# Operand splits of the fourth to sixth weight slab moved between the x parts at the start of three layers

## The chip, the cores and the metric

The kernel runs on one core of one Trainium2 chip. The metric is device time in microseconds (us) of one execution. Engines: TensorE (PE; its weight loads are PEld), VectorE (DVE), ScalarE (ACT), GpSimd (POOL) and the queue of SyncE (SP), which issues the loads.

## The reference, cut to what matters

Three blocks of token mixing alternate with three PEER layers (expert retrieval), over 256 tokens of width 1024. Each PEER layer begins with a norm of its input and a query projection; from the queries come scores against keys, the best 16 of each half, and then the experts' products.

```python
h = layer_norm(DN_ALPHA * h + mix, ln_g[layer, 0], ln_b[layer, 0])     # layers 0 and 1
ffn = peer(h, peer_w_q[layer], peer_sub_keys[layer], peer_u[layer], peer_v[layer])
...
h = h + peer_ffn(rmsnorm(h, g_ffn[l]), w_q[l], sub_keys[l], expert_u[l], expert_v[l])   # the third

q = (xt @ w_q).reshape(T, PEER_HEADS, 2, PEER_HALF)                    # 1024 x 2048 weights
```

The change lies wholly in the seam between the norm and `xt @ w_q`, in each of the three layers.

## The kernel before, in words

**Products.** Every fp32 product is made of three: an operand is split into a part `hi` (rounded to the matmul's format) and a rest `lo`, and hi\*hi, hi\*lo and lo\*hi are summed (`split_matmuls`, lines 598 to 600).

**Slabs.** All weights stream through a ring of three slots as slabs of 128 x 1024 (512 KB). A slab n goes through this chain: SyncE loads it into `ring` once the slot's previous `w_lo` is made (`put`, line 393); ScalarE makes `w_hi` (`split_lead`, line 903), once it is loaded and once slab n-3 is used up by TensorE (semaphore `used`); GpSimd or VectorE makes `w_lo = ring - w_hi` (`split_rest`, line 549); TensorE waits for `w_lo` (`slab_ready`). Which engine makes `w_lo` is written out by hand for each stretch: in the query slabs it is GpSimd, in `gpsimd_program`'s `peer`.

**A PEER layer's start.** The first eight query slabs (here slabs 0 to 7 of the layer) go through `wide`: slab c holds 128 rows of `w_q`, and x feature chunk c is the stationary operand. There are two tiles of 128 tokens, each with two halves of 512 columns, so a slab takes 6 products of 512 columns for one tile and 12 for both. `used` is raised when tile 1's products of the slab are done. Slabs 0 to 3 need features 0 to 511 of x (half 0), slabs 4 to 7 need half 1. Queries 8 to 15 come after them, with products of 256 columns.

**x.** The normed activations lie by token. TensorE turns them (a transpose through the identity, line 701, four for one part into a bank `acc`), ScalarE copies the part out as `x_hi` (`lead_x`, line 939), and VectorE makes `x_lo` (`rest_part`, line 1287). The four parts (tile, half) come in the order of `SKEW`: part 0 is (0,0), part 1 (1,0), part 2 (0,1), part 3 (1,1).

**The order before.** On TensorE (`skewed_queries`): turn part 0; slabs 0, 1 for tile 0; turn part 1; slab 2 for tile 0; slabs 0, 1, 2 for tile 1; turn parts 2 and 3; slab 3 and then slabs 4 to 7 for both tiles. On ScalarE (`finish`): `w_hi` of slabs 0 to 2 and `x_hi` of part 0, squares and standard deviation of tile 1, `x_hi` of parts 1, 2, 3, and only then (`peer`, `leads(first, DC)`) `w_hi` of slabs 3 and on. On VectorE (`skewed_layer_norm` in the first two layers, `skewed_rms` in the third): the norm's steps with `x_lo` of parts 0 and 1 between them, then `x_lo` of parts 2 and 3. On GpSimd: `w_lo` of slabs 0 to 15 in order. On SyncE (`sync_program`'s `peer`): slabs 0 to 5; then, once the whole input is normed, four loads of keys with three slabs after each. Every engine runs its own instructions in order.

Of the kernel before, what the change touches and what calls it, by code (L numbers as in the profile page):

```python
# [29 lines left out]
DC = D // P  # L30
# [4 lines left out]
SLOTS = 3  # L35
# [4 lines left out]
HP = 2 * HEADS  # L40
# [6 lines left out]
SKEW = ((0, 0), (1, 0), (0, 1), (1, 1))  # L47
# [505 lines left out]
def gpsimd_program(k, pool):  # L553
    def run(name, at, rounds):

        with pool.Fori(0, rounds) as i:
            for p in range(SLOTS):
                split_rest(k, pool, Slab(k.first[name] + at + p, i))

    def some(name, at, to):  # L560
        for n in range(at, to):
            split_rest(k, pool, Slab(k.first[name] + n))

    def stage(name, count):
        run(name, 0, count // SLOTS)
        some(name, count - count % SLOTS, count)

    def peer(layer):
        stage(f"qw{layer}", HP)
        u = f"u{layer}"  # L570
        run(u, 0, (EARLY + SLOTS) // SLOTS)
        some(u, (EARLY + SLOTS) // SLOTS * SLOTS, EARLY + SLOTS)

    for name in k.stages:
        if name[:4] == "peer":
            peer(int(name[4]))
        else:
            for part in PARTS_OF[name]:
                part = f"{name}_{part}"
                if part in ("ab_wide", "c_wide"):  # L580
                    continue
                if k.first[part]:
                    stage(part, k.count[part])
                else:
                    some(part, 1, k.count[part])
# [5 lines left out]
class Tensor:  # L591
# [100 lines left out]
    def skewed_queries(self, layer, src):  # L692

        k, pe, w = self.k, self.pe, self.w
        first, parts, banks = k.first[f"qw{layer}"], k.parts_before(f"peer{layer}"), k.query_banks()

        def turn(n):
            t, half = SKEW[n]
            pe.wait_ge(k.h_part, parts - 4 + n + 1)
            for c in range(4):  # L700
                ins = pe.transpose(k.acc[t * 2 + half][:, c * P:(c + 1) * P],
                                   src[t][:, (4 * half + c) * P:(4 * half + c + 1) * P], k.ident[:, :])
            ins.then_inc(k.xt, 1)

        def slabs(*chunks, tiles=range(NT)):
            for c in chunks:
                self.wide(Slab(first + c), c, banks, tiles=tiles)

        self.keep_busy(20)
        turn(0)  # L710
        self.keep_busy(12)
        w.next(k.x_ready)
        slabs(0, 1, tiles=[0])
        turn(1)
        slabs(2, tiles=[0])
        w.next(k.x_ready)
        slabs(0, 1, 2, tiles=[1])
        turn(2)
        turn(3)
        slabs(3)  # L720
        w.next(k.x_ready, 2)
        slabs(4, 5, 6, 7)
# [165 lines left out]
class Scalar:  # L888
# [78 lines left out]
    def tile_squares(self, t):  # L967
# [4 lines left out]
            self.square(k.h[:, t, half * 512:(half + 1) * 512], 2 * t + half)  # L972
        self.tile_std(t)

    def finish(self, name, end):

        k, act = self.k, self.act
        after = k.stages[k.stages.index(name) + 1:][:1]
        act.activation(k.small[:, 46:47], k.small[:, 47:48], ACT.Sqrt)
        if after == ("s",):  # L980
            self.w.next(k.meta, 16)
            self.square(MixS(k).meta, 2 * NT)
            self.tile_std(NT)
        self.split_lead(Slab(end))
        if name in RMS_AFTER:
            self.tile_squares(0)
            if after:
                self.split_lead(Slab(end + 1))
                self.split_lead(Slab(end + 2))
                self.lead_x([0], halves=[0])  # L990
            self.tile_squares(1)
            if after:
                for t, half in SKEW[1:]:
                    self.lead_x([t], halves=[half])
            return
        eps = k.small[:, 49:50]
        if after in (("peer0",), ("peer1",)):
            self.centred_squares(0)
            self.tile_std(0, eps)
            self.split_lead(Slab(end + 1))  # L1000
            self.split_lead(Slab(end + 2))
            self.lead_x([0], halves=[0])
            self.centred_squares(1)
            self.tile_std(1, eps)
            for t, half in SKEW[1:]:
                self.lead_x([t], halves=[half])
        elif after != ("s",):
            for t in range(NT):
                self.centred_squares(t)
            for t in range(NT):  # L1010
                self.tile_std(t, eps)
            self.split_lead(Slab(end + 1))
            self.lead_x([0])
            self.lead_x([1])
            self.split_lead(Slab(end + 2))
        else:
            for t in range(NT):
                self.centred_squares(t)
                if t:
                    self.tile_std(0, eps)  # L1020
                self.split_lead(Slab(end + 1 + t))
            self.tile_std(1, eps)
            self.lead_meta()
            for t in range(NT):
                self.tile_squares(t)
            self.lead_x(range(NT), at=META)

    def peer(self, layer):
# [20 lines left out]
            bank = k.query_bank(n)  # L1049
            self.column(Slab(first + n), q[:, n, :], src=None if bank is None else lambda _: bank[:, 0:T])  # L1050

        self.leads(first, DC)
        self.wide(first + DC - 1, [(k.query_banks()[t * 2 + half], q_tok[:, t, half * 512:(half + 1) * 512], ACT.Copy)
                                   for t in range(NT) for half in range(2)], k.q_tok)
        for n in range(DC, HP):
# [115 lines left out]
class Vector:  # L1171
# [118 lines left out]
    def skewed_layer_norm(self, slot, last):  # L1290
        k, dve, own = self.k, self.dve, self.own
        gain, bias = view(k.big, G_AT[slot], D), view(k.big, G_AT[slot] + D, D)
        means, squares, before = self.w.count(k.mean), self.w.count(k.sq), self.w.count(k.xhi)

        def residual(t, half):
            self.add_residual(t, half, last, DN_ALPHA, sums=True)

        def minus_mean(t):
            own.join()
            dve.tensor_scalar(k.small[:, 20 + t:21 + t], k.small[:, 16 + 2 * t:17 + 2 * t],  # L1300
                              k.small[:, 17 + 2 * t:18 + 2 * t], -1.0 / D, ALU.add, ALU.mult).then_inc(k.mean, 1)

        def centre(t, half):
            dve.wait_ge(k.mean, means + t + 1)
            dve.wait_ge(k.sq, squares + 2 * t + half + 1)
            acc = k.acc[t * 2 + half][:, :]
            own.do(dve.scalar_tensor_tensor(acc, acc, k.small[:, 20 + t:21 + t], gain[:, half * 512:(half + 1) * 512],
                                            ALU.add, ALU.mult))

        def variance(t):  # L1310
            dve.wait_ge(k.sq, squares + 2 * t + 2)
            dve.tensor_scalar(k.small[:, 4 + t:5 + t], k.small[:, 40 + 2 * t:41 + 2 * t],
                              k.small[:, 41 + 2 * t:42 + 2 * t], 1.0 / D, ALU.add, ALU.mult).then_inc(k.var, 1)

        def scale(t, half):
            cut, acc = slice(half * 512, (half + 1) * 512), k.acc[t * 2 + half][:, :]
            own.join()
            dve.scalar_tensor_tensor(k.h[:, t, cut], acc, k.small[:, 12 + t:13 + t], bias[:, cut], ALU.mult, ALU.add)\
               .then_inc(k.h_part, 1)

        residual(0, 0)
        residual(0, 1)
        minus_mean(0)
        residual(1, 0)
        self.w.next(k.param[slot], 32)
        centre(0, 0)
        variance(0)
        self.inverse_std(0)
        scale(0, 0)
        residual(1, 1)  # L1330
        minus_mean(1)
        self.rest_part(0, before)
        centre(1, 0)
        variance(1)
        self.inverse_std(1)
        scale(1, 0)
        centre(0, 1)
        self.rest_part(1, before)
        scale(0, 1)
        centre(1, 1)  # L1340
        scale(1, 1)
        self.rest_part(2, before)
        self.rest_part(3, before)
        self.w.skip(k.mean, 2)
        self.w.skip(k.sq, 4)
        self.w.skip(k.xhi, 4)
        self.w.skip(k.h_part, 4)

    def skewed_rms(self, last):
# [7 lines left out]
        def normed(t, half):  # L1357
            cut = slice(half * 512, (half + 1) * 512)
            dve.wait_ge(k.rms_in, parts + 2 * t + half + 1)
            dve.scalar_tensor_tensor(view(k.big, NORMED + t * D + half * 512, 512), k.h[:, t, cut],  # L1360
                                     k.small[:, 12 + t:13 + t], view(k.big, G_AT[0], D)[:, cut],
                                     ALU.mult, ALU.mult).then_inc(k.h_part, 1)
# [13 lines left out]
        normed(0, 1)  # L1376
        self.rest_part(1, before)
        normed(1, 1)
        self.rest_part(2, before)
        self.rest_part(3, before)  # L1380
        self.w.skip(k.rms_in, 4)
# [1674 lines left out]
```

## Time and profile before

| | us |
|---|---|
| median of 3 runs | 2921.48 |
| range of the runs | 2921.19 to 2923.51 |
| profiled execution, its own device time | 2923.99 |
| its span in the trace | 2922.2 |
| TensorE busy (99% of the span) | 2879.9 |
| VectorE busy (66%) | 1937.0 |
| ScalarE busy (54%) | 1564.6 |
| GpSimd busy (31%) | 894.1 |

The mean granted clock of TensorE over the span is 0.996. Times in the trace are us from the span's start. A timeline row gives start, duration, engine, line, operation, what it writes and reads, how often, and in brackets how long the engine stood idle before it and what ended that. L598, L599 and L600 are the three products of `split_matmuls`. A matmul's duration is longer than the distance to the next, because they overlap: the pace is read from the starts.

### The profile page before, as it was taken

The numbers are of one execution on the slowest core, as the hardware profiler recorded it, in microseconds if no ns is written. First come the engines' busy times: TensorE is split into PE (matmuls) and PEld (weight loads), VectorE is DVE, ScalarE is ACT, GpSimd is POOL, SyncE is SP. The second block draws the span as 40 slices with busy tenths as digits, with TensorE's granted clock in tenths as the row PEclk, the third lists the DMA queues.
The fourth block names the chain that finished last, engine by engine and source line by source line (L and its number), as shares of the span: only waits on it lengthen the run. The fifth ranks groups of instructions, "written<-read, shape, count | busy, mean of one in ns | idle before, by whom it ended". The sixth has DMA issues, their size and how long they took to land.

```text
span 2922.2 us, 59257 instructions
## 1 busy us (share of the span) xinstructions
PE 2879.9 (99%) x21307; PEld 2618.0 (90%) x21307; DVE 1937.0 (66%) x3382; ACT 1564.6 (54%) x2548; POOL 894.1 (31%) x361
## 2 busy tenths in 40 slices
PE   8999999999999999999999999999999999999999
PEld 7799999888888879999998888889799999988887
DVE  4379477788556636947778855675529667788655
ACT  4444544677555544454467744654554544477554
POOL 3679600000004367970000000255779820000000
PEclk9999999999999999999999999999999999999999
DMA  6556555555765455565555576433466555555664
GB/s 214 160 174 182 186 168 172 173 173 179 238 191 163 145 158 174 186 185 169 171 172 174 178 234 196 144 130 123 162 182 181 181 181 168 170 175 177 203 195 162
DMA packets 146462, 515.17 MB, mean 176 GB/s; under 512 B 17552, under 2 KB 18576, under 8 KB 146336
## 3 DMA queue, kind: packets, MB, share of 16 engines
q1 hardware_dynamic: 146336, 513.46, 56.0%
q8 instruction: 83, 1.36, 0.2%
q14 instruction: 43, 0.35, 0.0%
HBM read 509.20 MB, written 4.19 MB: 176 GB/s over the span
## 4 chain that ended last, share of the span: by engine, by line
PE 91%; POOL 2%; DVE 2%; ACT 2%; issue 2%; DMA 0%; SPq 0%; DVEq 0%; ACTq 0%; POOLq 0%
PE col L598 15%; PE col L600 15%; PE col L599 15%; PE acc L598 13%; PE acc L600 13%; PE acc L599 13%; POOL w_lo L549 2%; PE col L796 2%; PE acc L796 2%; PE acc L754 1%; ACT w_hi L903 1%; ACT work L963 0%; PE acc L2511 0%; PE misc L2524 0%; DVE work L1840 0%
## 5 line engine op out<-in xcount | busy, mean ns | idle before, releaser
L549 POOL TENSOR_TENSOR w_lo<-ring,w_hi 128x1024 fp32r<-128x1024 f32 x357 | 893.9, 2515 | 1461.3 <-ACT w_hi L903 1460.2
L903 ACT ACTIVATE w_hi<-ring 128x1024 fp32r<-128x1024 f32 x941 | 992.8, 1056 | 571.9 <-PE acc L600 449.2
L598 PE MATMUL col<-x_hi,w_hi 128*128 128x256 f32 (+1 forms) x3712 | 1051.8, 283 | 2.9 <-DVE x_lo L1192 1.7
L599 PE MATMUL col<-x_lo,w_hi 128*128 128x256 f32 (+1 forms) x3712 | 1045.3, 282 | 0.0
L600 PE MATMUL col<-x_hi,w_lo 128*128 128x256 f32 (+1 forms) x3712 | 1044.9, 281 | 0.0
L549 DVE TENSOR_TENSOR w_lo<-ring,w_hi 128x1024 fp32r<-128x1024 f32 x584 | 714.0, 1223 | 375.1 <-ACT w_hi L903 371.7
L598 PEld LDWEIGHTS col<-x_hi,w_hi 128*128 128x128 f32 x3712 | 701.4, 189 | 6.2 <-issue 3.3
L600 PEld LDWEIGHTS col<-x_hi,w_lo 128*128 128x128 f32 x3712 | 702.4, 189 | 0.0
L599 PEld LDWEIGHTS col<-x_lo,w_hi 128*128 128x128 f32 x3712 | 698.7, 188 | 0.7
L598 PE MATMUL acc<-w_hi,c_hi 128*128 128x512 f32 x1664 | 653.5, 393 | 1.0 <-issue 1.0
L600 PE MATMUL acc<-w_hi,c_lo 128*128 128x512 f32 x1664 | 648.2, 390 | 0.0
L599 PE MATMUL acc<-w_lo,c_hi 128*128 128x512 f32 x1664 | 647.4, 389 | 0.0
L910 ACT ACTIVATE work<-col 128x256 f32 (+1 forms) x431 | 166.0, 385 | 663.6 <-PE col L600 663.5
L600 PEld LDWEIGHTS acc<-w_hi,c_lo 128*128 128x128 f32 x1664 | 312.3, 188 | 66.1
L598 PEld LDWEIGHTS acc<-w_hi,c_hi 128*128 128x128 f32 x1664 | 312.5, 188 | 64.4 <-issue 1.5
L599 PEld LDWEIGHTS acc<-w_lo,c_hi 128*128 128x128 f32 x1664 | 312.6, 188 | 63.3
L1450 DVE TENSOR_TENSOR c_lo<-work,c_hi 128x256 fp32r<-128x256 f32 x390 | 165.2, 424 | 14.4 <-ACT c_hi L1097 14.1
L1097 ACT ACTIVATE c_hi<-work 128x256 fp32r (+1 forms) x384 | 153.6, 401 | 0.0
L1457 DVE MAX8 work<-work 128x8 f32<-128x128 f32 (+1 forms) x144 | 35.4, 322 | 161.4 <-ACT work L1038 161.1
L1583 DVE SCALAR_TENSOR_TENSOR work<-acc,work 128x512 f32 (+1 forms) x96 | 61.8, 686 | 99.9 <-PE acc L796 99.9
L1572 DVE TENSOR_TENSOR h_tok<-mask_i,pairs_of_gate 128x2048 f16<-128x2048 f16 x96 | 123.6, 1287 | 0.0
L1102 ACT ACTIVATE h_tok<-iota_fp,neg_i 128x128 f16<-128x128 f16 x384 | 121.9, 388 | 0.2
(326 smaller groups left out, 2184.5 us busy)
## 6 DMA issues: line engine op xcount, KB each, us to landing
ring<-in_u SPq DMA_DIRECT2D x384, 512.0 KB, 3.5
ring<-in_v SPq DMA_DIRECT2D x384, 512.0 KB, 3.5
ring<-in_qw SPq DMA_DIRECT2D x24, 512.0 KB, 3.5
ring<-in_wq SPq DMA_DIRECT2D x24, 512.0 KB, 3.6
ring<-in_s_in SPq DMA_DIRECT2D x21, 512.0 KB, 3.3
ring<-in_c_in SPq DMA_DIRECT2D x16, 512.0 KB, 3.6
ring<-in_s_out SPq DMA_DIRECT2D x16, 512.0 KB, 3.3
ring<-in_s_gate SPq DMA_DIRECT2D x12, 512.0 KB, 3.3
```

The source lines that it names most:

```text
L549: eng.tensor_tensor(k.w_lo[s.slot][:, :], k.ring[s.slot][:, :], k.w_hi[s.slot][:, :].bitcast(F32), ALU.subtract).then_inc(k.lo[s.slot], 1)
L598: pe.matmul(out, a[0], b[0], start=start, stop=False, **kw)
L599: pe.matmul(out, a[0], b[1], start=False, stop=False, **kw)
L600: return pe.matmul(out, a[1], b[0], start=False, stop=stop, **kw)
L796: ins = pe.matmul(banks[t // HALF][:, t % HALF * EARLY:(t % HALF + 1) * EARLY], k.oh1[:, t, :], k.oh2[:, n, t, :], start=n == 0, stop=n == ...
L903: act.activation(k.w_hi[s.slot][:, :], k.ring[s.slot][:, :], ACT.Copy).then_inc(k.hi[s.slot], 1)
L910: act.activation(dst, src, func).then_inc(k.evac, 1)
L1097: act.activation(k.c_hi[s.slot][:, :], act_of[:, s.index(values), :], ACT.Copy).then_inc(k.coef_h, 1)
L1102: act.activation(k.oh1[:, t, :], k.iota_b[:, :], ACT.Abs, bias=k.neg_i1[:, at])\
L1450: dve.tensor_tensor(k.c_lo[s.slot][:, :], src, k.c_hi[s.slot][:, :].bitcast(F32), ALU.subtract).then_inc(k.coef[s.slot], 1)
L1572: dve.tensor_tensor(k.oh2.rearrange("p n t (i two) -> p n t i two", two=2), mask.unsqueeze(1).to_broadcast(shape), k.gate[:, bass.ds(b.ind ...
L1583: ins = dve.scalar_tensor_tensor(part, banks[half][:, :].rearrange("p (t i) -> p i t", t=HALF), 1.0 / GATE_UNIT, part, ALU.mult, ALU.mult)
```

## The change

Four edits, the same in all three PEER layers.

- TensorE turns part 2 after slab 0's products for tile 1 (then slab 1), and part 3 after slab 1's (then slab 2), not both after slab 2's.
- ScalarE makes `w_hi` of slab 3 after `x_hi` of part 1, of slab 4 after part 2's and of slab 5 after part 3's (`leads_among_x`); `leads` in `peer` begins with slab 6 accordingly.
- VectorE makes `w_lo` of slab 3, between the last step of the norm and `x_lo` of part 2.
- GpSimd leaves slab 3 out; it makes slabs 0 to 2 and 4 to 15, written out rather than in a loop.

```diff
     def peer(layer):                                   # gpsimd_program
-        stage(f"qw{layer}", HP)
+        some(f"qw{layer}", 0, SLOTS)
+        some(f"qw{layer}", SLOTS + 1, HP)
...
         w.next(k.x_ready)                              # skewed_queries
-        slabs(0, 1, 2, tiles=[1])
+        slabs(0, tiles=[1])
         turn(2)
+        slabs(1, tiles=[1])
         turn(3)
+        slabs(2, tiles=[1])
         slabs(3)
         w.next(k.x_ready, 2)
         slabs(4, 5, 6, 7)
...
+    def leads_among_x(self, end):                      # Scalar
+        for n, (t, half) in enumerate(SKEW[1:]):
+            self.lead_x([t], halves=[half])
+            self.split_lead(Slab(end + SLOTS + n))
...
-            for t, half in SKEW[1:]:                   # finish, at both places
-                self.lead_x([t], halves=[half])
+            self.leads_among_x(end)
...
-        self.leads(first, DC)                          # Scalar.peer
+        self.leads(first + SLOTS, DC - SLOTS)
...
         scale(1, 1)                                    # skewed_layer_norm
+        split_rest(k, dve, Slab(last + 1 + SLOTS))
         self.rest_part(2, before)
...
         normed(1, 1)                                   # skewed_rms
+        split_rest(k, dve, Slab(last + 1 + SLOTS))
         self.rest_part(2, before)
```

## Rows read from the trace of the kernel before

**Rows 1.** The page: busy us, share of the span and instructions of each engine
```profile
PE 2879.9 (99%) x21307; PEld 2618.0 (90%) x21307; DVE 1937.0 (66%) x3382; ACT 1564.6 (54%) x2548; POOL 894.1 (31%) x361
```
**Rows 2.** TensorE's waits over the span: us in total, times, longest
```profile
PE col L598 <- POOL w_lo L549: 13.2, 7, 4.1
```
**Rows 3.** Timeline of TensorE, first PEER layer
```profile
100.88 0.60 PE L701 MATMUL acc<-ident,h_tok 128*128 128x128 f32 x4
101.23 0.48 PE L598 MATMUL col<-w_hi,x_hi 128*128 128x512 f32 x1
101.55 0.39 PE L599 MATMUL col<-w_lo,x_hi 128*128 128x512 f32 x1
...
104.38 0.40 PE L598 MATMUL col<-w_hi,x_hi 128*128 128x512 f32 x1
...
107.18 1.03 PE L701 MATMUL acc<-ident,h_tok 128*128 128x128 f32 x8
...
112.33 0.79 PE L598 MATMUL col<-w_hi,x_hi 128*128 128x512 f32 x1 [4.11 <-POOL w_lo L549]
...
128.77 0.28 PE L598 MATMUL acc<-x_hi,w_hi 128*128 128x256 f32 x1
```
**Rows 4.** Timeline of ScalarE, same layer
```profile
107.82 1.08 ACT L939 ACTIVATE x_hi<-acc 128x512 fp32r<-128x512 f32 x2 [5.71 <-PE acc L701]
108.79 2.95 ACT L903 ACTIVATE w_hi<-ring 128x1024 fp32r<-128x1024 f32 x3
117.85 1.06 ACT L903 ACTIVATE w_hi<-ring 128x1024 fp32r<-128x1024 f32 x1 [6.11 <-PE misc L600]
```
**Rows 5.** Timeline of VectorE and GpSimd, same layer
```profile
104.19 0.75 DVE L1318 SCALAR_TENSOR_TENSOR h_tok<-acc,small,work 128x512 f32<-128x512 f32 x1
108.45 1.29 DVE L1287 TENSOR_TENSOR x_lo<-acc,x_hi 128x512 fp32r<-128x512 f32 x2 [3.50 <-ACT x_hi L939]
...
95.82 4.73 POOL L549 TENSOR_TENSOR w_lo<-ring,w_hi 128x1024 fp32r<-128x1024 f32 x2 [4.08 <-ACT w_hi L903]
109.92 7.00 POOL L549 TENSOR_TENSOR w_lo<-ring,w_hi 128x1024 fp32r<-128x1024 f32 x3 [9.37 <-ACT w_hi L903]
118.99 2.40 POOL L549 TENSOR_TENSOR w_lo<-ring,w_hi 128x1024 fp32r<-128x1024 f32 x1 [2.06 <-ACT w_hi L903]
```
**Rows 6.** Windows of one core: length; busy of PE, PEld, DVE, ACT, POOL; PEclk; DMA; GB/s
```profile
112.33:117.61 5.28, 5.28 (x12) 4.12 (x13) 0.00 (x0) 0.00 (x0) 4.60 (x2) 0.50 0.67 195
117.61:128.77 11.16, 11.16 (x50) 9.09 (x49) 0.00 (x0) 4.25 (x4) 8.63 (x4) 0.99 0.62 178
```
**Rows 7.** Timeline of TensorE, second and third PEER layer
```profile
1064.65 1.04 PE L701 MATMUL acc<-ident,h_tok 128*128 128x128 f32 x8
1069.79 0.61 PE L598 MATMUL col<-w_hi,x_hi 128*128 128x512 f32 x1 [4.11 <-POOL w_lo L549]
1085.32 0.28 PE L598 MATMUL acc<-x_hi,w_hi 128*128 128x256 f32 x1
...
2115.66 1.03 PE L701 MATMUL acc<-ident,work 128*128 128x128 f32 x8
2120.80 0.50 PE L598 MATMUL col<-w_hi,x_hi 128*128 128x512 f32 x1 [4.11 <-POOL w_lo L549]
2136.32 0.28 PE L598 MATMUL acc<-x_hi,w_hi 128*128 128x256 f32 x1
```
**Rows 8.** VectorE's `w_lo` (ns, least, median, most); landing of loads; last query load
```profile
L549 DVE TENSOR_TENSOR w_lo<-ring,w_hi x584: 1210/1226/1229, 10.8 to 2908.3; 128x1024 fp32r<-128x1024 f32 x195
...
DMA to landing us min/median/max: 3.3/3.5/4.4
...
2100.07 8.13 SPq L393 DMA_DIRECT2D ring<-in_qw  x3
```
**Rows 9.** Routing of the first layer: VectorE's timeline, and the chain that ended last
```profile
184.46 2.28 DVE L1482 TENSOR_TENSOR work<-work 128x2048 f32<-128x2048 f32 x1
...
184.81 4.20 POOL w_lo L549
```

## What was predicted

> **What bounds the kernel now.** I read first the page's busy times: TensorE is busy 99% of the span [rows 1]. That says that only time in which TensorE stands, or runs slowly, can be won without removing products. Then TensorE's waits, longest first: one entry towers over the rest, waits for GpSimd's `w_lo` in query products, 13.2 us in seven pieces of up to 4.1 [rows 2]. The timeline tells where: three pieces of 4.11 us, one at the start of each PEER layer, before the first product of slab 3 [rows 3, 7]. The other four pieces share the 0.9 us left.
>
> What the reader is to see around the wait at 112.33 in the first layer: TensorE ends slabs 0 to 2 and turns parts 2 and 3 from 107.18 on [rows 3]. Only then can ScalarE copy both parts, and it splits slab 3 behind them, from 108.79 [rows 4]; GpSimd makes its `w_lo` from 109.92 and needs some 2.4 us [rows 5]. So the wait is a chain, transposes, `x_hi`, `w_hi`, `w_lo`, and not the want of an engine: slabs 3 to 5 could have been split earlier. GpSimd was idle for 9.37 us before it [rows 5], ScalarE for 5.71 us before the x copies [rows 4].
>
> The wait costs more than itself. The 12 products after it took 5.28 us at a granted clock of 0.50, which is 1.2 GHz; the 48 of slabs 4 to 7 took 11.16 us at 0.99, practically 2.4 GHz, that is 2.79 us a slab [rows 6]. TensorE had stood for 4.11 us before the slow stretch [rows 3].
>
> **The change part by part.** I rebuild the first layer's seam from 104.38, where slab 0's six products for tile 1 are issued [rows 3]; nothing before that moves, since up to there each engine has the same instructions.
>
> *TensorE.* A turn between products: it begins at 100.88 where the next product would have begun, that one begins at 101.23, and its successor after 0.32 in place of about 0.23 [rows 3]; so a turn costs 0.35 + 0.09 = 0.44, say 0.45 us. Six products take 1.40 us. Then: turn part 2 from 104.38, slab 1 from 104.83, turn part 3 from 106.23, slab 2 from 106.68, slab 3 from 108.08. Before, two adjacent turns after 107.18 would have ended at about the same point, so splitting them costs nothing that I count; the bounds are 0 and 0.45 us a layer, for an extra entry and exit.
>
> *ScalarE.* A slab's `w_hi` begins 0.24 us after the product of the next slab begins (windows change slab at 117.61, ScalarE begins at 117.85) [rows 4, 6], and takes 1.06. Slab 3: released by slab 0 at 104.38, so 104.62 to 105.68. `x_hi` of part 2 follows at once, to about 106.2. Slab 4: slab 1 ends at 106.23, so 106.47 to 107.53; `x_hi` of part 3 to about 108.1; slab 5: released at 108.08, so 108.32 to 109.38. These are the same five instructions as now [rows 4], moved into idle time; they lie beside TensorE's products.
>
> *VectorE.* The norm's last step ends at 104.94 [rows 5]; the new `w_lo` of 1.23 us [rows 8] waits for `w_hi` of slab 3 and runs from about 105.72 to 106.95. Queued behind it are `x_lo` of parts 2 and 3, 1.29 us for both [rows 5]: the first to about 107.6, the second, after its `x_hi`, to about 108.8. TensorE wants them for slab 4 only, at 110.87: 2 us to spare. The added wait thus holds up nobody.
>
> *GpSimd.* Without slab 3 it starts slab 4 at about 107.6. Three splits took 7.00 us [rows 5], so 2.36 for one of a row: 107.6 to 110.0, and slab 5 to 112.35. TensorE wants slab 3 at 108.08 and gets it at 107.0 (1.1 us to spare), slab 4 at 110.87 (0.8), slab 5 at 113.66 (1.3). That the loop is written out is costed at nothing: it lies in GpSimd's idle time.
>
> *SyncE.* Load 6 waits for `w_lo` of slab 3, now 107.0 in place of 112.3, and stands behind the first key load and the wait for the normed input, both untouched and over before it (the norm ends at 104.94). Loads land 3.3 to 4.4 us after issue [rows 8], here by 111.4; ScalarE could take slab 6 at 108.08 + 2.79 + 0.24 = 111.11. At worst its `w_lo` is then 0.3 us later than by `used`, 115.1, and wanted at 116.45. Load 7 follows `w_lo` 4: issued 110.0, landed by 114.4, split on both engines by 117.9, wanted at 119.24. From then on GpSimd's 2.4 us stand against 2.79 a slab, with 1.7 to 1.9 us to spare, as now.
>
> *Clock.* No pause longer than a turn's 0.45 us is left from slab 0 for tile 1 to query 8, so I count slab 3 at 2.79 us in place of 5.28. No row shows this exact mix of turns and products, but the twelve products from 104.38 to 107.18 are at full pace, right behind a stretch with a turn in it [rows 3]. Bounds: the slow stretch wholly kept, or wholly gone.
>
> The sum. Query 8 begins five slabs after slab 3, 13.95 us.
> First layer: 108.08 + 13.95 = 122.03 against 128.77 [rows 3]: 6.74.
> Second: both turns begin at 1064.65, so slab 3 at 1065.55 and query 8 at 1079.50, against 1085.32 [rows 7]: 5.82.
> Third: 2115.66 + 0.90 + 13.95 = 2130.51 against 2136.32 [rows 7]: 5.81. Here VectorE is at the same point of its work, and the last load of slabs 3 to 5 was issued at 2107.9 [rows 8], landed by 2112.3, wanted at about 2116.8.
> Together 18.4 us; of it 12.7 is standing still (4.25 a layer) and 5.6 the clock (2.49, 1.58, 1.57). The profiled execution took 2923.99: 2905.6 after. The median of the runs, 2921.48, lies 2.5 lower, so 2903.1. Behind the seam all work hangs on TensorE's own progress (scores, routing, `used`), so I let it shift as a block: routing starts as much earlier as slab 51, which needs its result.
>
> *A lock between VectorE and GpSimd.* The first layer's routing shows one: a VectorE operation with both inputs in SBUF ran from 184.46 to 186.74, and GpSimd's `w_lo` begun at 184.81 took 4.20 us in place of 2.4, that is 1.8 more, about the overlap [rows 9]. The new VectorE split has two such inputs. By my times GpSimd is idle under it (last split over at 100.55 [rows 5], next at 107.6), so it costs nothing.
> The Trainium skill (SBUF — State Buffer, Who interferes with whom) has this as a rule that speaks against giving VectorE this work: an instruction with two SBUF inputs and a GpSimd instruction that reads SBUF exclude each other for the whole instruction, and whoever comes second waits. By that rule the trace agrees, 1.8 us at 184.81; and if the two did meet here, GpSimd would lose up to 1.23 us, which is the rival priced below.
>
> **The rivals.**
> (a) *A smaller wait takes its place.* Slack is 0.8 to 1.3 us for slabs 3 to 5, built from handoffs read elsewhere. If GpSimd's slab 4 came 1.23 us late, by the lock or by slow handoffs, TensorE would wait 0.4 us a layer; with 0.45 for dearer turns and something on slab 3 the loss is 0.5 to 1.5 a layer, 1.5 to 4.5 in all: 2904.6 to 2907.6. For it: thin slack. Against: nothing overlaps.
> (b) *The wait goes, the clock falls all the same* (each slow stretch of 1.6 to 2.5 us kept): 5.6 less, 2908.7. Against: the pace was full up to 107.18 with a turn among the products [rows 3].
> (c) *The gain is given back later*, where something doesn't follow TensorE; about half, 2912. Against: later waits on GpSimd are 0.9 us in all [rows 2].
> (d) *The splits don't come earlier*, because ScalarE meets slab 3 before it is loaded or `used` comes too late: about 2921. The loads speak against it.
> (e) *Slower.* ScalarE works in order, and `x_hi` of parts 2 and 3 now stand behind the splits of slabs 3 and 4, which wait for their loads; before, they stood behind no load. The place is load 4 of the third layer: issued before load 5, so by 2107.9 [rows 8], landed by 2112.3 at the slowest landing, and wanted by ScalarE at 2115.0 (106.47 moved by the distance of the double turns, 2115.66 - 107.18). If it lands D after that, slab 4 comes D - 0.8 late; the gain of 5.8 is eaten from D = 6.6, a landing nearly 14 us after issue against the 4.4 seen. At 16 us in each layer some 2 us a layer are lost: 2927. Nothing in the trace comes near.
>
> **How the numbers follow.** Forecast 0.72; (a) 0.14; (b) 0.05; (c) 0.04; (d) 0.02; (e) 0.03. The predicted time is the forecast's, 2903.1. The range takes in (a), and (b) nearly: 2909. Below, some 3 us: runs spread by 2.3 us, and the clock may cost nearer to 2.5 in all three layers in the timed runs (1.8 more): 2900. A measurement of this kernel can tell about 0.2% (5.8 us) from no change. (a) to (c) are all faster by more than that, so faster 0.95, within 0.2% 0.02, slower 0.03.
>
> **What would show it.** Right: the three 4.1 us waits gone; VectorE's slab 3 split 1.23 us long with GpSimd idle beside it; slab 3 right behind slab 2, at about 108.1, 4.25 us earlier than now; granted clock at 0.99 or more from slab 3 to slab 7; query 8 at about 122.0; the spans between later landmarks unchanged. Wrong: a wait on `w_lo` of slab 4 or 5 or on `x_lo`; a GpSimd split over 3 us in the seam; a clock of 0.50 after it; load 6 in ScalarE's way; or a new wait near slab 51.

## The result, and the profile after

| | before | after |
|---|---|---|
| median of the runs shown with the result, us | 2922.49 (4 runs, 2921.19 to 2924.95) | 2904.86 (4 runs, 2901.65 to 2907.28) |
| profiled execution, us | 2923.99 | 2906.76 |
| its span, us | 2922.2 | 2905.0 |

The ratio is 0.9938, with a 95% interval of 0.9921 to 0.9955: 0.6% faster. Repeated later beside other runs of the kernel before, it was 0.9924 (0.9908 to 0.9941). The executions compared below are the profiled ones. One of all the timed runs, of the variant "Both turns after slab 0", was in a slow state (4040.18 us at a mean granted clock of 0.654), and that variant's ratio is of its other three runs.

In the changed kernel the three products stand on lines 599 to 601, the turn on 702, `w_hi` on 906, `x_hi` on 942, `x_lo` on 1294.

TensorE's waits over the whole span, longest in total first (us in total, times, longest), of the changed kernel:

```profile
PE acc L688 <- DMA h_tok<-in_x: 6.4, 1, 6.4
PE acc L2488 <- ACT work L2596: 2.4, 1, 2.4
PE col L599 <- DVE w_lo L549: 2.4, 3, 1.3
PE col L657 <- DVE h_tok L1256: 2.0, 1, 2.0
...
PE col L599 <- POOL w_lo L549: 1.6, 5, 0.8
```

The entry of 13.2 us with pieces of 4.1 [rows 2] has shrunk to 1.6 with none over 0.8. The 2.4 us on VectorE's `w_lo` (1.1 in the profile before) lie ahead of the first seam, as does the 0.8 us piece on GpSimd's, and no seam shows a wait.

The first seam on TensorE's timeline, changed kernel (start, duration, engine, line, operation, operands, count):

```profile
104.47 0.50 PE L599 MATMUL col<-w_hi,x_hi 128*128 128x512 f32 x1
...
105.97 0.60 PE L702 MATMUL acc<-ident,h_tok 128*128 128x128 f32 x4
106.32 0.48 PE L599 MATMUL col<-w_hi,x_hi 128*128 128x512 f32 x1
106.64 0.40 PE L600 MATMUL col<-w_lo,x_hi 128*128 128x512 f32 x1
...
107.81 0.60 PE L702 MATMUL acc<-ident,h_tok 128*128 128x128 f32 x4
108.16 0.47 PE L599 MATMUL col<-w_hi,x_hi 128*128 128x512 f32 x1
...
109.63 0.39 PE L599 MATMUL col<-w_hi,x_hi 128*128 128x512 f32 x1
...
123.46 0.28 PE L599 MATMUL acc<-x_hi,w_hi 128*128 128x256 f32 x1
```

It answers to [rows 3]: the turns stand at 105.97 and 107.81, slab 3 begins at 109.63 with no wait, and query 8 at 123.46. The first line is slab 0's first product for tile 1, which before was at 102.89. So all of this seam lies 1.58 us later than in the profile before. That comes from ahead of the seam (see "The whole change again"), so distances are what can be compared.

The other engines in the same seam, answering to [rows 4, 5]:

```profile
106.17 1.06 ACT L906 ACTIVATE w_hi<-ring 128x1024 fp32r<-128x1024 f32 x1 [2.47 <-PE misc L601]
107.13 0.58 ACT L942 ACTIVATE x_hi<-acc 128x512 fp32r<-128x512 f32 x1
108.00 1.06 ACT L906 ACTIVATE w_hi<-ring 128x1024 fp32r<-128x1024 f32 x1 [0.29 <-PE misc L601]
108.97 0.58 ACT L942 ACTIVATE x_hi<-acc 128x512 fp32r<-128x512 f32 x1
109.83 1.06 ACT L906 ACTIVATE w_hi<-ring 128x1024 fp32r<-128x1024 f32 x1 [0.28 <-PE misc L601]
...
107.26 1.22 DVE L549 TENSOR_TENSOR w_lo<-ring,w_hi 128x1024 fp32r<-128x1024 f32 x1 [0.73 <-ACT w_hi L906]
...
109.14 7.13 POOL L549 TENSOR_TENSOR w_lo<-ring,w_hi 128x1024 fp32r<-128x1024 f32 x3 [7.00 <-ACT w_hi L906]
```

ScalarE's five instructions alternate, VectorE's split takes 1.22 us and ends at 108.48, 1.15 us before TensorE wants it, and GpSimd begins with slab 4 only at 109.14.

Two windows of the changed kernel (length; busy of PE, PEld, DVE, ACT, POOL; granted clock; DMA share; GB/s), slabs 3 to 7 in the first and third layer, which answer to [rows 6]:

```profile
109.63:123.46 13.83, 13.83 (x62) 11.28 (x61) 0.64 (x1) 5.31 (x5) 12.88 (x6) 1.00 0.67 215
2105.50:2119.35 13.85, 13.85 (x62) 11.28 (x61) 0.65 (x1) 5.31 (x5) 12.89 (x6) 1.00 0.72 214
```

The granted clock is 1.00 (2.4 GHz) throughout; the stretch at 0.50 (1.2 GHz) is gone.

**Where the time went.** I call *seam* the distance from slab 0's first product for tile 1 to query 8.

| seam, us | before | after | less |
|---|---|---|---|
| first layer | 102.89 to 128.77: 25.88 | 104.47 to 123.46: 18.99 | 6.89 |
| second | 1060.35 to 1085.32: 24.97 | 1055.06 to 1074.04: 18.98 | 5.99 |
| third | 2111.39 to 2136.32: 24.93 | 2100.35 to 2119.35: 19.00 | 5.93 |
| sum | | | 18.81 |

The stretches between the seams change little: from query 8 of the first layer to the second seam 931.58 before and 931.60 after, from there to the third 1026.07 and 1026.31, and from the last query 8 to the end of the span 785.9 and 785.7. The spans differ by 17.2: 18.8 in the seams, less the 1.58 ahead of the first one.

### The profile page after: what moved, and what is told of

Its sections match the earlier page's. It is cut to its first block, busy times and chain, and to the rows that moved or that the text cites. A ratio compares the mean times of both kernels' runs of the same rounds, so it can differ in the third digit from the quotient of the medians.

```text
span 2905.0 us, 59209 instructions
## 1 busy us (share of the span) xinstructions
PE 2873.3 (99%) x21307; PEld 2613.4 (90%) x21307; DVE 1938.4 (67%) x3385; ACT 1565.1 (54%) x2548; POOL 888.5 (31%) x358
## 4 chain that ended last, share of the span: by engine, by line
PE 92%; DVE 2%; ACT 2%; POOL 2%; issue 1%; DMA 0%; DVEq 0%; SPq 0%; ACTq 0%; POOLq 0%
PE col L599 15%; PE col L601 15%; PE col L600 15%; PE acc L599 13%; PE acc L601 13%; PE acc L600 13%; POOL w_lo L549 2%; PE col L799 2%; PE acc L799 2%; PE acc L757 1%; ACT w_hi L906 1%; ACT work L966 0%; PE acc L2520 0%; PE misc L2533 0%; DVE work L1849 0%
## 5 line engine op out<-in xcount | busy, mean ns | idle before, releaser
L1466 DVE MAX8 work<-work 128x8 f32<-128x128 f32 (+1 forms) x144 | 35.4, 322 | 145.7 <-ACT work L1045 145.4
```

## The experiments

Each kernel was profiled once, and its seams are read as above. Ratios are to the kernel before, run beside it. The ratios of the variants lie close together, and several can't be told apart by them; what separates them is the length of the seams, which the unchanged repetition below gave again within 0.02 us.

**The turns alone.** The kernel before with TensorE's new order only:

```diff
-        slabs(0, 1, 2, tiles=[1])
-        turn(2)
-        turn(3)
+        slabs(0, tiles=[1])
+        turn(2)
+        slabs(1, tiles=[1])
+        turn(3)
+        slabs(2, tiles=[1])
```

> The kernel before, with the new order on TensorE alone (part 2 turned after slab 0, part 3 after slab 1); the splits of slabs 3 to 5 stay behind x_hi of part 3, and GpSimd makes slab 3's w_lo. I call seam the distance from slab 0's first product for tile 1 to query 8: 25.88, 24.97 and 24.93 us in the three layers before, 18.98 after the whole change. Theory (the splits' place sets the wait): x_hi of part 3 now ends near 107.6 on the clock of rows 3, w_hi of slab 3 near 108.7, w_lo near 111.1, so slab 3 still waits some 3.0 us in place of 4.25 and the seam is 22.0 if the clock stays up, 23.5 to 24.5 if it falls. Total 3 to 9 us faster than before. Rival (the turns' place brings the gain): seams of 19 to 20, 15 us or more faster.

Measured: seams of 23.50, 23.54 and 21.94, ratio 0.9975 (0.9965 to 0.9984), median 2916.36 against 2924.81. The slabs' splits still stand behind `x_hi` of part 3. Windows from slab 3 to query 8 of its first and third layer (the second one starts 0.08 us before slab 3, which begins at 2115.43):

```profile
110.42:125.93 15.51, 15.51 (x60) 12.58 (x61) 0.00 (x0) 4.25 (x4) 13.24 (x6) 0.89 0.65 191
2115.35:2129.37 14.02, 13.95 (x60) 11.39 (x61) 0.00 (x0) 4.25 (x4) 13.38 (x7) 1.00 0.72 214
```

```profile
110.42 0.79 PE L598 MATMUL col<-w_hi,x_hi 128*128 128x512 f32 x1 [2.66 <-POOL w_lo L549]
111.01 0.63 PE L599 MATMUL col<-w_lo,x_hi 128*128 128x512 f32 x1
```

The same wait of 2.66 us stands in all three layers. Behind it the clock fell in the first two (the products go at 0.43 us instead of 0.23), not in the third, and 15.51 against 13.94 us from slab 3 to query 8 is the price, 1.6 us. So the theory holds in size (22.0 with the clock up, 23.5 with the fall): this part takes 1.4 to 3.0 us from a seam, 6.8 in all.

**The splits alone.** The changed kernel with the old order of turns:

```diff
-        slabs(0, tiles=[1])
-        turn(2)
-        slabs(1, tiles=[1])
-        turn(3)
-        slabs(2, tiles=[1])
+        slabs(0, 1, 2, tiles=[1])
+        turn(2)
+        turn(3)
```

> The changed kernel with TensorE's old order: parts 2 and 3 both turned after slab 2. ScalarE's w_hi of slab 4 then stands behind x_hi of part 2, which is turned only near 107.7. Theory: slab 3 is ready in time (its split stands ahead of part 2), slab 4's w_lo comes at about 111.8 and is wanted at 110.87, a wait of about 0.9 us, no fall of the clock: seams of 19.9, total some 16 us faster than before, 2.8 slower than the whole change. Rival (the turns are needed for the gain): slabs 4 and 5 each wait 2 us or more and seams are over 22.

Measured: seams of 20.27, 20.27 and 20.26, ratio 0.9951 (0.9935 to 0.9968). The chain from a late `x_hi` of part 2 to slab 4's split is there as expected, once a layer (slab 4 begins at 111.50):

```profile
106.70 1.04 PE L702 MATMUL acc<-ident,h_tok 128*128 128x128 f32 x8
111.50 0.47 PE L599 MATMUL col<-w_hi,x_hi 128*128 128x512 f32 x1 [1.01 <-POOL w_lo L549]
...
107.70:122.68 14.98, 13.97 (x61) 11.08 (x60) 1.38 (x2) 6.86 (x8) 12.82 (x6) 1.00 0.57 188
```

A wait of 1.01 us, and the clock stays at 1.00; the seams are 0.37 us longer than expected, on the theory's side. Of the 18.8 us of the whole, the splits alone (ScalarE's place for three of them and VectorE's share together) give 15.0 (5.61 + 4.70 + 4.67); the turns then add 3.8. In the other order the turns give 6.8 and the splits add 12.0, so 3 us of the gain come with whichever part is made first. The total of the timed runs fell by 15.7.

**GpSimd makes the fourth slab's `w_lo`.** The changed kernel without VectorE's share:

```diff
-        some(f"qw{layer}", 0, SLOTS)
-        some(f"qw{layer}", SLOTS + 1, HP)
+        some(f"qw{layer}", 0, HP)
...
-        split_rest(k, dve, Slab(last + 1 + SLOTS))
```

> The changed kernel, but GpSimd makes slab 3's w_lo as before and VectorE doesn't. Theory (GpSimd had room): its splits run slab 3 until about 1.1 us later than VectorE's, just when TensorE wants it (wait 0 to 0.2 us), slab 4 until 0.4 us ahead of need, slab 5 0.8 ahead; seams 19.0 to 19.3, total within 1 us of the whole change. Rival (VectorE's 1.22 us in place of GpSimd's 2.4 matters): a wait of 1 us or more at slab 3 or 4, seams of 20 or more.

Measured: seams of 19.22, 19.23 and 19.21, as expected; ratio 0.9939 (0.9922 to 0.9955), which the timing doesn't tell from the whole change. GpSimd's splits run without a pause from slab 3 on:

```profile
108.46 11.90 POOL L549 TENSOR_TENSOR w_lo<-ring,w_hi 128x1024 fp32r<-128x1024 f32 x5 [5.17 <-ACT w_hi L905]
```

With everything else of the change in place, VectorE's part is worth 0.24 us a layer. The rival, that without it TensorE waits 1 us or more, fell. What VectorE's part is worth under the old order of turns wasn't tried.

**The wait filled.** The kernel before, its order and its splits untouched, with fillers where TensorE waits:

```diff
         turn(3)
+        ones = k.ident[:, :].bitcast(BF16)
+        for _ in range(36):
+            pe.matmul(k.acc[0][:, 0:2 * P], ones[:, 0:P], ones, start=True, stop=True)
         slabs(3)
```

> The kernel before, with 36 filler products of 256 columns in bf16 (about 3.9 us, results unused) between the turn of part 3 and slab 3, in each layer: the wait for slab 3's w_lo stays, but TensorE isn't idle in it. Theory (the idle time makes the clock fall): granted clock 1.00 through slab 3, whose twelve products take 2.8 us; seams 23.35 in all three layers, so 2.5, 1.6 and 1.6 us less than before, total 5.6 us faster, and the other 13 us of the change are the wait itself. Rival (the clock falls for another reason, the turns or the mix): a stretch at 0.50 stays and the total is within 1.5 us of before.

Measured: seams of 23.38, 23.99 and 24.25, so 2.50, 0.98 and 0.68 less than before, 4.2 in all; ratio 0.9982 (0.9972 to 0.9992), median 2919.55 against 2924.81. The granted clock is 1.00 in every window of 4 us that I read in its three seams. The first layer came out as expected, the others missed by 0.6 and 0.9. In the third:

```profile
2114.85 4.09 PE L722 MATMUL acc<-ident 128*128 128x256 bf16 x36
2119.13 0.50 PE L598 MATMUL col<-w_hi,x_hi 128*128 128x512 f32 x1 [0.19 <-POOL w_lo L549]
2131.08 0.50 PE L598 MATMUL col<-w_hi,x_hi 128*128 128x512 f32 x1 [0.60 <-POOL w_lo L549]
...
2122.72 1.06 ACT L906 ACTIVATE w_hi<-ring 128x1024 fp32r<-128x1024 f32 x1 [4.19 <-DMA ring<-in_qw]
2127.51 1.06 ACT L906 ACTIVATE w_hi<-ring 128x1024 fp32r<-128x1024 f32 x1 [3.73 <-DMA ring<-in_qw]
```

With the clock up, TensorE reached slab 7 before its `w_lo`, because ScalarE had waited for the loads of slabs 6 and 7, which are issued only when `w_lo` of slabs 3 and 4 is made. How long slab 7's load took to land decided it: 3.7 us in the first layer, where no wait followed, 5.7 in the second (a wait of 0.33 us) and 6.0 in the third (0.60). Those two waits are part of the misses of 0.6 and 0.9; the rest wasn't traced. So idle time is what the fall of the clock hangs on in this seam, and undoing the fall without moving the splits leaves little room for a late load.

**The whole change again.**

> The changed kernel once more, to see what differs between executions. Theory: the three seams are again 18.98 us within 0.05, and what moves is the stretch before the first seam (slab 0's first product for tile 1 began at 102.89 in the kernel before and at 102.4 to 105.6 in the others so far); the total lies 18 to 19 us below the kernel before beside it. Rival: the seams themselves vary by 0.5 us or more.

Measured: seams of 18.99, 18.98 and 18.99, ratio 0.9924 (0.9908 to 0.9941), median 2903.03 against 2925.12. The seams repeat within 0.02 us. Most of what moves lies ahead of the first one: slab 0's first product for tile 1 began at 104.35, and over the ten profiles at 101.47 to 105.64. Two stretches in it move, and the profiles give both. The start of the kernel to the first wide product of the first mixer ends at 35.4 to 37.2; it holds short waits on `w_lo`, while loads of the first 40 us took up to 7.7 us to land. And that mixer's stretch to its output products takes 29.6 us at a mean clock of 1.00 in one execution, 31.0 to 31.7 at 0.94 or 0.95 in six, 32.4 to 32.6 at 0.90 in three.

The traces show where in that stretch the clock falls. The changed kernel's first profile:

```profile
59.89 4.49 PE L1778 MATMUL acc<-work 32*128 32x256 f32 x32
60.00:70.00 10.00, 10.00 (x50) 8.31 (x51) 4.11 (x10) 2.09 (x3) 3.06 (x2) 0.83 0.40 110
```

TensorE makes 32 products that fill only 32 of its 128 rows, without a pause, and the granted clock is at 0.50 from about 65 to 68.4 us, right behind them or, in other profiles, from their last microseconds on. It fell there in nine of the ten profiles, for 3 to 7 us, and not in the tenth, with no wait in front of it.

A second place moves too. From query 8 of the second layer to the third seam it is 1024.6 to 1024.9 us in three profiles ("Both turns after slab 0", "The engines swapped", "One split early"), 1026.1 to 1026.4 in six and 1026.7 in the filled one. Two waits of TensorE lie in it, of 2.00 and 2.44 us: behind the first the clock fell in the three short profiles and the filled one, behind the second in all but those three.

**Both turns after slab 0.** The changed kernel with

```diff
         slabs(0, tiles=[1])
         turn(2)
-        slabs(1, tiles=[1])
         turn(3)
-        slabs(2, tiles=[1])
+        slabs(1, 2, tiles=[1])
```

> The changed kernel with parts 2 and 3 both turned after slab 0 (then slabs 1 and 2). Theory (each entry into a turn costs TensorE 0.35 us at the switch and 0.09 at the product behind it, so two adjacent turns cost a little less than two single ones): seams 0.1 to 0.2 us shorter than 18.98 if the input's last part is normed in time (it was 0.2 us before the turn would begin), total within 1 us of the whole change. Rival: TensorE waits for the norm's last step, or used for slab 1 comes later and slab 4's w_lo with it (0.45 us later, slack 0.8): seams of 19.0 to 19.4.

Measured: seams of 19.25, 19.25 and 19.01, ratio 0.9931 (0.9911 to 0.9950). The expected gain of 0.1 to 0.2 us isn't there, and the rival's first half is right for the two layers with a layer norm:

```profile
105.08 1.28 PE L702 MATMUL acc<-ident,h_tok 128*128 128x128 f32 x8
106.12 0.48 PE L599 MATMUL col<-w_hi,x_hi 128*128 128x512 f32 x1
```

Eight transposes take 1.28 us where two turns otherwise take 1.03 [rows 3]: part 3 isn't normed when its turn is due (VectorE's last step of the norm runs from 104.90 to 105.65, the turns begin at 105.08). In the third layer the eight take 1.04, and together costs what apart costs.

**The engines swapped.** The changed kernel with GpSimd on slab 3 and VectorE on slab 4, so that the two splits overlap:

```diff
-        some(f"qw{layer}", 0, SLOTS)
-        some(f"qw{layer}", SLOTS + 1, HP)
+        some(f"qw{layer}", 0, SLOTS + 1)
+        some(f"qw{layer}", SLOTS + 2, HP)
...
-        split_rest(k, dve, Slab(last + 1 + SLOTS))
         self.rest_part(2, before)
+        split_rest(k, dve, Slab(last + 2 + SLOTS))
```

> The changed kernel with GpSimd making w_lo of slab 3 and VectorE that of slab 4 (between x_lo of parts 2 and 3), so that the two splits overlap: GpSimd's from 105.8 to 108.1, VectorE's ready to start near 107.6 (times as in the prediction). Theory (operations with both inputs in SBUF on the two engines exclude each other): one of the two is longer in the trace by about the overlap of 0.5 us (VectorE 1.7 in place of 1.22, or GpSimd 2.9 in place of 2.4), and seams are 18.9 to 19.4. Rival (no exclusion): 1.22 and 2.36 us side by side.

Measured: seams of 19.28, 19.23 and 19.26, ratio 0.9936 (0.9920 to 0.9953).

```profile
106.75 1.69 DVE L549 TENSOR_TENSOR w_lo<-ring,w_hi 128x1024 fp32r<-128x1024 f32 x1 [0.66 <-ACT w_hi L906]
...
104.95 2.40 POOL L549 TENSOR_TENSOR w_lo<-ring,w_hi 128x1024 fp32r<-128x1024 f32 x1 [5.16 <-ACT w_hi L906]
```

GpSimd's split ran to 107.35, undisturbed; VectorE's, begun at 106.75, took 1.69 us, 0.47 more than its usual 1.22, most of the 0.60 of overlap. The one that came second paid, here VectorE, in [rows 9] GpSimd: either engine can be the one that pays.

**One split early.** The changed kernel with only slab 3's split among the x parts:

```diff
-            self.split_lead(Slab(end + SLOTS + n))
+            if n == 0:
+                self.split_lead(Slab(end + SLOTS))
...
-        self.leads(first + SLOTS, DC - SLOTS)
+        self.leads(first + 1, DC - 1)
```

> The changed kernel with only slab 3's split among the x parts; w_hi of slabs 4 and 5 comes after x_hi of part 3, as in the kernel before. Theory (most of the gain hangs on slab 3): w_hi of slab 4 ends about 1.4 us later, w_lo near 111.4 against 110.8 wanted, a wait of 0.6 us at slab 4, none at slab 5; seams of 19.6, total some 2 us slower than the whole change and 16 faster than before. Rival (all three are needed): slab 5 waits too and seams are 21 or more.

Measured: seams of 19.34, 19.31 and 19.32, ratio 0.9931 (0.9914 to 0.9947). A loss of 0.33 us a layer, half of what was expected. ScalarE:

```profile
103.17 1.06 ACT L906 ACTIVATE w_hi<-ring 128x1024 fp32r<-128x1024 f32 x1 [2.47 <-PE misc L601]
104.13 0.58 ACT L942 ACTIVATE x_hi<-acc 128x512 fp32r<-128x512 f32 x1
105.44 0.60 ACT L942 ACTIVATE x_hi<-acc 128x512 fp32r<-128x512 f32 x1 [0.73 <-PE acc L702]
105.93 2.00 ACT L906 ACTIVATE w_hi<-ring 128x1024 fp32r<-128x1024 f32 x2
```

`w_hi` of slab 4 ends at 106.99; against slab 3's at 104.23 that is 2.76 later, where the whole change has 1.83 (107.23, 109.06). So it is 0.93 later, not 1.4, because part 3's copy needn't wait behind slab 4's split and comes earlier itself.

## Why the prediction was right, point by point

The result, 2904.86 us, lies in the range of 2900.0 to 2909.0 and 1.8 us above the predicted 2903.1. By the median alone it would also fit rival (a), 2904.6 to 2907.6; it is the seams that decide for the forecast.

**What binds.** Right: the chain from the transposes to slab 3's `w_lo` set the wait. The turns alone left 2.66 us of it before slab 3, the splits alone moved it to slab 4 and left 1.01, both together left none.

**TensorE's order.** Predicted with the 1.58 us shift added: second turn at 107.81, slab 3 at 109.66, query 8 at 123.61. Measured: 107.81, 109.63, 123.46. A single turn cost 0.45 us as read off [rows 3] (105.97 to 106.32, then 0.32 to the next product). The bound of 0.45 us a layer for dearer split turns wasn't used: from the first turn to the second it is 1.84 us, counted as 1.85.

**ScalarE, VectorE, GpSimd.** Predicted, again with the shift: `w_hi` of slab 3 at 106.20, of slab 4 at 108.05, of slab 5 at 109.90; `w_lo` of slab 3 ending at 108.53; GpSimd from 109.2. Measured: 106.17, 108.00, 109.83, 108.48, 109.14. The slack of slab 3 was as said (1.15 us for 1.1), and the kernel with GpSimd on slab 3 shows it from the other side: it used up what there was and lost only 0.24 us a layer.

**The seams.** Predicted 6.74, 5.82 and 5.81, measured 6.89, 5.99 and 5.93: the sum was 18.4 against 18.8. The missing 0.4 is the five slabs, 13.95 us by the pace of [rows 6] and 13.83 in fact: the window from which I took it, at a mean clock of 0.99, still had the last of the slow stretch in it (0.95 in its first 1.39 us, 1.00 behind that).

**The clock.** Right that it stays up, and the filled wait shows that in this seam idle time is the condition: same transposes, same order, no idle, no fall. It isn't the only one in this kernel, as the fall without a wait in the first mixer shows. And its share isn't simply 5.6 us that anyone could collect: alone it gave 4.2, as slab 7's load bound next in two layers. In the sum this doesn't show, since the earlier splits also bring the loads forward (`w_lo` of slab 3 by 5.4 us relative to the seam's start: 4.0 after it, 9.4 before).

**The median.** This is the term that was off. I carried the 18.4 us over to a median of three runs, 2921.48, and took the runs to spread by 2.3 us. Over 19 and 7 further runs the kernel before had medians of 2924.81 and 2925.12 and a spread of 5.7 us; the changed one had 2904.86 (beside 2922.49) and 2903.03 (beside 2925.12). The two differences, 17.6 and 22.1 us, stand on either side of the 18.8 of the seams. In the profiles, what moves is above all the stretch ahead of the first seam, which begins anywhere in 4.2 us, and some 1.5 us between the second and the third. The profiled pair drew 1.58 of the first the wrong way, so "nothing before that moves" holds for the instructions and not for the time. That the timed runs differ by the same two places is likely and not shown, since they left no traces.

**The rivals.** A smaller wait in its place: none in the whole change. The clock falling all the same, the gain given back later, slower: no sign; the stretches between seams kept their length within 0.3 us in the compared pair. The splits held up by a late load: not in the three seams, but the slowest landing that I reckoned with, 4.4 us, isn't the slowest there is, as the 6.0 us of the filled wait show. The lock between VectorE and GpSimd is real, as the swapped engines show, and cost nothing here because GpSimd was idle: VectorE's split runs from 107.26 to 108.48, GpSimd's next begins at 109.14.

The Trainium skill (SBUF — State Buffer, Who interferes with whom) has the second comer wait for the whole instruction of the first; the trace agrees in kind, with 0.47 us paid on an overlap of 0.60.

**What stays open.** Why the clock falls behind the 32 small products in nine profiles and not in the tenth, and for differing lengths, wasn't tried; nor why the same wait brings a fall in one execution and not in another. None of the variants has a seam shorter than the whole change by more than the 0.02 us of repetition, and the seam is now products and two turns without a pause, so no further version was built.

## What to carry to other kernels

When an engine at 99% waits for a chain of short steps on engines that stand idle before it, look for the step in program order that keeps the chain from starting: here three splits made earlier gave 12 to 15 of 19 us, and which engine made one of them gave 0.7, with the rest in place. Rebuild such a seam step by step on the trace's own clock, handoffs included; it held within 0.15 us here. And compare distances between landmarks inside the kernel rather than totals: the seams repeated within 0.02 us where totals moved by up to 5.7.

## What the runs showed of the hardware that was not expected

- A wait of 2.66 us on TensorE was followed by a fall of the granted clock to 0.50 in two of three seams and not in the third, with the same kind of instructions around it. Behind waits of 4.11 us it fell in all three seams, behind waits of 1.01 us in none. Elsewhere in the kernel, a wait of 2.00 us was followed by a fall in four of ten profiles, one of 2.44 us in seven. The price of a fall in a seam was 1.6 to 2.6 us.
- The clock also fell with no wait at all: behind 32 products on 32 of the 128 rows, 4.5 us long, in nine of ten profiles.
- A slow stretch can hide a later bound: with the wait filled and the clock at 1.00, waits of 0.33 and 0.60 us on a later slab appeared that the kernel before didn't have.
